# Stick-breaking sums as two passes of rounded values on TensorE, one weight group further on

## The reference

```python
z = jnp.einsum('bhqc,bhkc->bhqk', qh[:, :, t0:t1], kh[:, :, :t1]).astype(jnp.float32) * scale
before = s_idx < t_idx
log_keep = jnp.where(before, jax.nn.log_sigmoid(-z), 0.0)
between = lax.cumsum(log_keep, axis=3, reverse=True) - log_keep
a = jnp.where(before, jnp.exp(jax.nn.log_sigmoid(z) + between), 0.0)
outs.append(jnp.einsum('bhqk,bhkc->bhqc', a.astype(vh.dtype), vh[:, :, :t1]))
```

## Time and profile before

| | |
|---|---|
| median of 3 runs | 822.16 us (822.06 to 822.74) |
| the profiled execution, its own time | 822.13 us |
| its span, first to last instruction | 820.1 us |
| PE busy | 811.2 us (99%) |
| DVE busy | 642.5 us (78%) |
| ACT busy | 520.1 us (63%) |
| PE on the chain of work that ended last | 96% |

### The profile page before, as it was taken

One profiled execution on the slowest core, in us unless ns is written; L12 is line 12 of the kernel. 1 busy time (PEld: TensorE's weight loads), 2 busy tenths in 40 slices (PEclk: granted clock), 3 DMA queues, 4 the chain that ended last, 5 costly groups with the idle time before them and its releaser, 6 DMA issues.

```text
span 820.1 us, 12037 instructions
## 1 busy us (share of the span) xinstructions
PE 811.2 (99%) x4604; PEld 698.8 (85%) x4604; DVE 642.5 (78%) x1129; ACT 520.1 (63%) x809; POOL 29.2 (4%) x54
## 2 busy tenths in 40 slices
PE   8999999999999999999999999999999999999997
PEld 5988988889888888888899889888988888888885
DVE  6899986776676899997387999848678489999753
ACT  6656885666557777765365488656666477776541
POOL 2100000010010000000010000001000000000000
PEclk9999999999999999999999999999999999999999
DMA  8755345473474565557666443446535545555751
GB/s 310 275 183 174 104 131 170 138 264 97 151 239 141 160 205 199 182 187 218 191 215 233 142 149 123 136 153 212 199 126 176 187 129 180 192 175 198 226 184 51
DMA packets 40444, 145.69 MB, mean 178 GB/s; under 512 B 4594, under 2 KB 4738, under 8 KB 40388
## 3 DMA queue, kind: packets, MB, share of 16 engines
q1 hardware_dynamic: 38448, 138.38, 51.8%
q0 software_dynamic: 1936, 6.55, 2.3%
q10 hardware_dynamic: 4, 0.00, 0.0%
HBM read 143.87 MB, written 1.05 MB: 177 GB/s over the span
## 4 chain that ended last, share of the span: by engine, by line
PE 96%; DMA 1%; issue 1%; DVE 1%; ACT 0%; SPq 0%; DVEq 0%; POOLq 0%; POOL 0%
PE acc L1619 8%; PE acc L1585 5%; PE acc L1587 5%; PE acc L1586 5%; PE psCD L1619 4%; PE acc L1629 4%; PE acc L1602 4%; PE acc L1682 4%; PE psAB L1619 4%; PE acc L1684 4%; PE acc L1683 4%; PE acc L1603 3%; PE acc L1604 3%; PE psAB L1586 3%; PE psAB L1585 3%; PE psAB L1587 3%
## 5 line engine op out<-in xcount | busy, mean ns | idle before, releaser
L955 DVE TENSOR_TENSOR wlo<-raw,whi 128x1024 fp32r<-128x1024 f32 x240 | 288.0, 1221 | 72.5 <-ACT whi L544 70.7
L544 ACT ACTIVATE whi<-raw 128x1024 fp32r<-128x1024 f32 x240 | 249.7, 1057 | 120.4 <-PE acc L1587 45.8
L1619 PE MATMUL acc<-xT,whi 128*128 128x512 f32 x288 | 89.0, 390 | 0.0
L1619 PEld LDWEIGHTS acc<-xT,whi 128*128 128x128 f32 x288 | 54.1, 188 | 11.8
L1473 DVE SCALAR_TENSOR_TENSOR KT<-V,par,KT 128x255 f32<-128x255 f32 (+1 forms) x144 | 59.9, 479 | 2.1 <-ACT KT L888 1.5
L1629 PE MATMUL acc<-xT,wlo 128*128 128x256 f32 x288 | 58.0, 283 | 0.0
L1602 PE MATMUL acc<-xT,whi 128*128 128x256 f32 x176 | 50.9, 289 | 0.0
L1235 DVE SCALAR_TENSOR_TENSOR arena<-arena,par 128x256 f32<-128x256 f32 x120 | 50.2, 479 | 0.8 <-ACT arena L740 0.8
L1619 PE MATMUL psCD<-xT,whi 128*128 128x512 f32 x160 | 50.0, 393 | 0.0
L1603 PE MATMUL acc<-xT,whi 128*128 128x256 f32 x176 | 49.7, 282 | 0.0
L1604 PE MATMUL acc<-xT,wlo 128*128 128x256 f32 x176 | 49.7, 282 | 0.0
(11 more groups left out here) (312 smaller groups left out, 2044.8 us busy)
## 6 DMA issues: line engine op xcount, KB each, us to landing
raw<-stream_dram SPq DMA_DIRECT2D x256, 512.0 KB, 4.1
gpost<-gain_dram POOLq DMA_DIRECT2D x6, 512.0 KB, 5.3
gpre<-gain_dram POOLq DMA_DIRECT2D x5, 512.0 KB, 6.9
memn<-mem_dram SPq DMA_DIRECT2D x2, 512.0 KB, 10.0
out_dram<-h SPq DMA_DIRECT2D x4, 256.0 KB, 2.1
cst<-const_dram SPq DMA_DIRECT2D x1, 896.0 KB, 6.3
h<-x_dram SPq DMA_DIRECT2D x2, 256.0 KB, 2.9
h<-x_dram SPq DMA_DIRECT2D x1, 512.0 KB, 7.2
```

Of the source, the lines that this page charges most:

```text
L544: act.activation(home(g)[0], raw[:, s * GW:(s + 1) * GW], ACT.Copy).then_inc(w_hi.sem, 1)
L955: dve.tensor_tensor(lo, raw[:, cols], hi.bitcast(F32), ALU.subtract).then_inc(w_lo.sem, 1)
L1619: e = pe.matmul(up_halves(j, c), whi[:, cols], both, start=k == 0, stop=k == KC - 1)
```

## The change

It does four things.

1. The sums over keys are formed from rounded operands. ACT copies the softplus to `sp_hi` (type fp32r, `keep_hi`), DVE subtracts to get `sp_lo` (`keep_lo`), and PE multiplies first `sp_hi`, then `sp_lo`, with the constants, which ACT has copied once, in layer 0, to a rounded `signs`. So PE has twelve products a pair where it had six.
2. On PE, the sums of pair 0 stand one weight group later, after the third group of WK1, and the scores of pair 1 after the fourth.
3. On ACT, `keep_hi(0)` stands ahead of `mixed_hi(7)`, and `keep_hi(1)` ahead of the split of WV0's last group. On DVE, `keep_lo(0)` stands after the split of WK1's fourth group, `sb_between(0)` one split later, and `keep_lo(1)` between the split of WV0's last group and the last taps.
4. Taps 25 to 31 are placed anew: none between `sb_between(0)` and `sb_masked(1)`, four behind `sb_masked(1)`, two at the end.

```diff
+        sp_lo = nc.alloc_sbuf_tensor_at("sp_lo", [P, 2 * AW], F32R, offset=sb_at + 2 * AW * 4)
+        sp_hi = nc.alloc_sbuf_tensor_at("sp_hi", [P, 2 * AW], F32R, offset=sb_at + 3 * 2 * AW * 4)
+        signs = nc.alloc_sbuf_tensor_at("signs", [P, 2 * P], F32R, offset=base + (ARENA - 2 * P) * 4)
...
-        tri = cst[:, CC_TRI:CC_TRI + P]
-        ones = cst[:, CC_ONE:CC_ONE + P]
+        tri = signs[:, 0:P]
+        ones = signs[:, P:2 * P]
...
+                def keep_hi(c):
+                    act.wait_ge(sp_ready.sem, sp_ready.at(l, c + 1))
+                    act.activation(sp_hi[:, :], sp, ACT.Copy).then_inc(sp_hi_in.sem, 1)
...
                 split(G_DLV + 3 + AHEAD)
+                if not l:
+                    act.wait_ge(cst_in.sem, 16)
+                    act.activation(signs[:, :], cst[:, CC_TRI:CC_TRI + 2 * P], ACT.Copy).then_inc(signs_in.sem, 1)
                 act.wait_ge(w_used.sem, w_used.at(l, G_DLV + PER_TILE))
...
                 split(G_WK1 + AHEAD)
+                keep_hi(0)
                 mixed_hi(7, o_done, 4, attended)
...
                 transposed_in(KT[:, 4 * SEQ:8 * SEQ], [a[:, :] for a in accs[0]], G_WK1 + PER_TILE, KT_in)
+                keep_hi(1)
                 split(G_WV0 + 1 + AHEAD)
...
+                def keep_lo(c):
+
+                    dve.wait_ge(sp_hi_in.sem, sp_hi_in.at(l, c + 1))
+                    dve.tensor_tensor(sp_lo[:, :], sp, sp_hi[:, :].bitcast(F32), ALU.subtract).then_inc(sp_lo_in.sem, 1)
...
                 split(G_WK1 + AHEAD)
+                keep_lo(0)
                 mixed_lo(4, 7, attended)
                 split(G_WK1 + 1 + AHEAD)
                 conv_taps(23, 25)
+                split(G_WK1 + 2 + AHEAD)
                 sb_between(0)
-                split(G_WK1 + 2 + AHEAD)
-                conv_taps(25, 26)
                 split(G_WK1 + 3 + AHEAD)
                 sb_masked(1)
-                conv_taps(26, 30)
+                conv_taps(25, 29)
                 sb_keep(1)
                 split(G_WV0 + AHEAD)
-                conv_taps(30, CV_K)
+                keep_lo(1)
+                conv_taps(29, CV_K)
                 split(G_WV0 + 1 + AHEAD)
...
-                    pe.wait_ge(sp_ready.sem, sp_ready.at(l, c + 1))
-                    for r in range(2):
-                        k = sp[:, r * AW:(r + 1) * AW]
-                        pe.matmul(psAB[r][:, 0:SEQ], tri, k[:, 0:SEQ], start=True, stop=False)
-                        pe.matmul(psAB[r][:, P:SEQ], ones, k[:, SEQ:AW], start=False, stop=True)
-                        e = pe.matmul(psAB[r][:, SEQ:AW], tri, k[:, SEQ:AW], start=True, stop=True)
+                    for landed, keep in ((sp_hi_in, sp_hi), (sp_lo_in, sp_lo)):
+                        first = landed is sp_hi_in
+                        pe.wait_ge(landed.sem, landed.at(l, c + 1))
+                        for r in range(2):
+                            k = keep[:, r * AW:(r + 1) * AW]
+                            pe.matmul(psAB[r][:, 0:SEQ], tri, k[:, 0:SEQ], start=first, stop=False)
+                            pe.matmul(psAB[r][:, P:SEQ], ones, k[:, SEQ:AW], start=False, stop=False)
+                            e = pe.matmul(psAB[r][:, SEQ:AW], tri, k[:, SEQ:AW], start=False, stop=not first)
                     e.then_inc(b_done.sem, 1)
...
-                transposed_product(G_WK1 + 1, 1, M, acc[0], k0=2)
-                pe.wait_ge(cst_in.sem, 16)
+                transposed_product(G_WK1 + 1, 2, M, acc[0], k0=2)
+                pe.wait_ge(signs_in.sem, 1)
                 sb_between(0)
-                transposed_product(G_WK1 + 2, 1, M, acc[0], k0=4)
+                transposed_product(G_WK1 + 3, 1, M, acc[0], k0=6)
                 pe.wait_ge(t_ready.sem, t_ready.at(l, 1))
                 sb_scores(1)
-                transposed_product(G_WK1 + 3, 1, M, acc[0], k0=6)
```

More of the change, by code:

```diff
@@ L202, in hybrid_trunk @@
         gpad = part(2 * (CV_K - 1 + SEQ)).rearrange("p (c n) -> p c n", c=2)
+        part(4)
         cacc = part(2 * SEQ)
@@ L207, in hybrid_trunk @@
         zs, sp, tt = (sb_a[:, i * 2 * AW:(i + 1) * 2 * AW] for i in range(3))
+        sb_at = base + taken[0] * 4 - 4 * 2 * AW * 4
+        sp_lo = nc.alloc_sbuf_tensor_at("sp_lo", [P, 2 * AW], F32R, offset=sb_at + 2 * AW * 4)
+        sp_hi = nc.alloc_sbuf_tensor_at("sp_hi", [P, 2 * AW], F32R, offset=sb_at + 3 * 2 * AW * 4)
+        signs = nc.alloc_sbuf_tensor_at("signs", [P, 2 * P], F32R, offset=base + (ARENA - 2 * P) * 4)
         qr, kr = sb_a[:, 0:TOK * NT], sb_a[:, TOK * NT:2 * TOK * NT]
@@ L218, in hybrid_trunk @@
         pT = part(2 * AW).rearrange("p (h n) -> p h n", h=2)
+        assert taken[0] + 2 * P <= ARENA
         sb_w = [a.rearrange("p c n -> p (c n)")[:, 0:2 * AW] for a in (dqT, dkT)]
@@ L363, in hybrid_trunk @@
         sp_ready = signal("sp_ready", 2)
+        sp_hi_in = signal("sp_hi_in", 2)
+        sp_lo_in = signal("sp_lo_in", 2)
+        signs_in = signal("signs_in", 0, before=1)
         b_done = signal("b_done", 2)
```

## The result

Measured in turn on the same chip: the changed kernel 834.11 us (median of 4, 833.04 to 834.47), the kernel before 822.35 (median of 4). The ratio is 1.0138, with an interval of 1.0127 to 1.0150: 1.4% slower, where 0.9% was forecast. The profiled execution took 834.18, its span is 832.1.

A forecast was written before the change was run, and what follows sets the result against it. PE, always busy, was taken as the bound, made to wait by the DVE and ACT chain. 3.8 to 3.9 us per layer, twice, gave 7.7 on 822.13, so 829.8, range 826.5 to 833.5.

The forecast's parts named there:

- the cost of the clock behind the stall: PE's clock after its waits in each layer: nothing in the sum, left to a rival at 8%.
- Steps 1 to 9, the chain on DVE and ACT: Each layer, pair 0's sums to the transposes: added operations queue up, transposes start at 127.2 or 127.3, +3.8 us.
- the three waits forecast on PE: PE idle before the values of pair 0 (1.6 us), the second pass of pair 1 (2.5) and the transposes (1.1).
- That neither end moves the result: PE's sums over keys: a call gains 0.7 or loses 0.5 us, but PE's time does not end the stretch.
- the 819.4 that the prediction gives for it: Time on PE alone, four calls of sums at 1.0 us for 1.67, -2.7 in all.
- The copy on ACT: The added 128x768 copy of softplus to `sp_hi`, for each pair: 0.82 us.
- The rival "the stall makes the clock fall": Behind the stall PE's clock drops to its lower level: 2.8 us more a layer, 835.4; chance 8%.
- do not tell: Windows of before have PE never standing still, at clock 1.00, so they do not show a stall's effect on it.
- the likeliest case: Both layers delayed by the chain, 7.7 us in all: 829.8, own range 828.2 to 831.4, chance 74%.
- no other new idle time: Profile sign: PE idle only before pair 0's values, pair 1's second pass and the transposes.

The follow-up runs named there:

- the waits filled: Changed kernel plus idle products on PE, 9 ahead of the wait for the copy of `KT` and 18 between pair 1's two passes: 830.61 us, ratio 1.0096.
- the kernel with `KT` first: Changed kernel with one move: ACT copies `KT` ahead of the softplus of pair 1 instead of behind it; 834.10 us, ratio 1.0142.
- both removed: Changed kernel plus idle products in PE's two longest waits and 8 one-column memsets more on DVE in each layer: 830.12 us, ratio 1.0092.
- the reordered kernel: Changed kernel with `KT` copy and weight splits earlier on ACT, taps and splits moved on DVE, a weight group moved ahead on PE: 822.48 us, ratio 0.9997.

## Why the prediction was wrong

It gave 829.8 and 826.5 to 833.5; measured were 834.1. The direction was right, but of the 12.0 us (834.1 - 822.1) only 7.7 were forecast. The chain itself cost 7.3 (3.6 a layer); 3.4 came from the clock, 1.0 from the end and 0.2 from the start of the span. The term that failed is the cost of the clock behind the stall, which the sum put at nothing and left to a rival.

- **Steps 1 to 9, the chain on DVE and ACT: right.** The last taps end at 127.26 (forecast 127.2), `KT` is copied by 121.70 (121.63), the second subtraction starts at 124.73 (124.65). Without the clock a layer loses 3.6 (37.88 - 34.25), forecast 3.8. Of the three waits forecast on PE (1.6, 2.5 and 1.1) two are there, with 1.1 and 2.2. The third, ahead of the transposes, is not there in the changed kernel, and is 0.3 with the waits filled. Two things make it shorter than forecast: the second pass takes longer than the 0.5 put (0.7 at the full clock, 1.34 at the lower one), and the first transpose waits only for the taps of its half of the channels (`conv_done` is signalled for each half), not for the very last tap. That more than one thing must move to gain anything is borne out by the kernel with `KT` first.
- **"That neither end moves the result": right.** A call of rounded products takes 1.32 us (109.75 to 111.07), not 1.0. The products of 128 columns go at 0.06 (109.87 to 109.93), but the last of each three takes 0.12, and the next of 256 then 0.16. The gain of a call is 0.35 to 0.37, not 0.7. It was luck that this did no harm: the stall covered it. In the kernel before, one float32 product of 256 columns takes 0.43 us (106.66 to the next line), against 0.12 for a rounded one, 3.6 times as long:

```profile
107.09 0.38 PE L1760 MATMUL psAB<-arena,cst 128*128 128x128 f32 x2
```

The Trainium skill ("FP8 and Floating Point Precision", section "TensorE Precision Notes") has a float32 product in four passes; the trace is near that for the single product, and yet the call of twelve is 0.8 of the old one (1.32 against 1.67), not half. By half the passes, a call would take 0.84 and the time would be 818.8, an estimate from the page's four passes; the 819.4 that the prediction gives for it goes by the call of 1.0.

- **The copy on ACT: right.** 0.83 and 0.84, forecast 0.82. The Trainium skill ("ScalarE: Activation LUTs", section "What ACT_TABLE_LOAD costs") gives 186 ns and 0.833 ns an element for an instruction with immediate scale and bias, by which I estimate 0.83 for 768; the trace agrees.
- **The rival "the stall makes the clock fall", at 8%: it happened,** in both layers, for 1.9 and 1.5 us. The step that failed is this chance, and with it the zero for the clock in the sum. I wrote that the windows of before "do not tell", and then left 3.4 us out of the likeliest case all the same, where a trace without any idle PE gives no ground for a small chance. The price given for it (2.8 a layer, 835.4) was somewhat high: by the 0.58 in the window from 128 to 132 the clock was low until about 131.4 (an estimate), 4.3 us behind the start of the transposes at 127.07. At half the speed that loses some 2.1 us; measured were 1.9.
- **Nothing was said of the end.** 1.0 us came with a fetch of instructions that no row of before shows, because it was not there. It belongs with "no other new idle time" and was missing from the sum.

With both removed, the same chain gives 829.7. That this meets 829.8 so closely is in part luck: in that profiled execution the two stages make 7.2 of the 8.0 us that the span is longer, and most of the rest is 0.5 more ahead of the stage of layer 0 and 0.4 between the two stages.

## What to carry to other kernels

Where two engines hand work to each other in turn, a delay in one of them arrives whole at the end of the chain, and a wait taken away in the middle buys nothing (834.10 against 834.11): follow the chain to the last thing that the bound engine waits for. Put the early and independent work (here `KT`, a weight split, some taps) into the gaps that the handovers leave; in this case that turned a loss of 1.4% into no loss, and with the end cured into a gain of 0.14%. In this kernel a wait of 2.2 us on PE lowered the clock in both layers, one of 1.7 us in one layer of two, and one of 1.1 us alone in neither. When a forecast has PE standing still that long in a kernel where it never did, add the price of the clock to the likeliest case instead of to a rival.

## What I had not expected

Idle products made the kernel faster by 3.5 us (834.1 to 830.6), by keeping the clock at its upper level through a wait of 2.2 us. And 16 useless memsets on DVE made the reordered kernel 1.1 to 1.3 us faster (822.3 or 822.5 to 821.2); a fetch of instructions then no longer fell among the last output packets.
